# Expert gate rows from one-hot tables: float32 marks and one weighted product per token, against 16-bit marks and three products per token

## The reference, cut to what matters

```
q      = h @ wq                                  # 8 heads x 2 halves x 128
s1, s2 = q_half @ keys[head, half].T             # 128 key scores for each half
top 16 of s1, top 16 of s2; 256 sums; top 16 of the sums per head
w      = softmax(those 16 sums)                  # per head
expert = 128 * key1 + key2                       # 16384 experts, 128 picks per token
out    = sum over picks of  w * gelu(h . u[expert]) * v[expert]
```

## Time and profile before

| | before |
|---|---|
| median of 3 runs | 4277.51 us (4276.9 to 4279.27) |
| span of the profiled execution | 4272.1 us |
| TensorE matmul busy in it | 4130.4 us, 97% |
| VectorE busy in it | 3026.6 us, 71% |
| ScalarE busy in it | 1804.8 us, 42% |
| mean share of the DMA engines, query and selection tiles of the first call (1550 to 1720 us) | 0.67 |

### The profile page before, as it was taken

One profiled execution on the slowest core, in us unless ns is written; L12 is line 12 of the kernel. 1 busy time (PEld: TensorE's weight loads), 2 busy tenths in 40 slices (PEclk: granted clock), 3 DMA queues, 4 the chain that ended last, 5 costly groups with the idle time before them and its releaser, 6 DMA issues. The chain is left out here.

```text
span 4272.1 us, 80920 instructions
## 1 busy us (share of the span) xinstructions
PE 4130.4 (97%) x30455; PEld 3777.3 (88%) x30455; DVE 3026.6 (71%) x5239; ACT 1804.8 (42%) x2677; POOL 32.3 (1%) x54
## 2 busy tenths in 40 slices
PE   9999999999997899999999999999998899999999
PEld 9978999879895699999888899998886699999887
DVE  5566565565525479787888697878885579787888
ACT  4344343343324344444333444443333444444333
POOL 0000000000000000000000000000000000000000
PEclk9999999999999999999999999999999999999999
DMA  6534656436320157545776465457771156546776
GB/s 241 215 147 168 232 201 229 148 137 229 131 89 21 60 178 226 189 176 196 234 234 214 176 229 191 174 187 235 234 234 68 60 203 221 187 176 202 233 235 199
DMA packets 299140, 783.66 MB, mean 183 GB/s; under 512 B 33008, under 2 KB 132336, under 8 KB 298352
## 3 DMA queue, kind: packets, MB, share of 16 engines
q1 hardware_dynamic: 298864, 779.78, 53.4%
HBM read 728.27 MB, written 51.38 MB: 182 GB/s over the span
## 5 line engine op out<-in xcount | busy, mean ns | idle before, releaser
L262 ACT ACTIVATE ring_hi<-ring 128x1024 fp32r<-128x1024 f32 x1173 | 1244.7, 1061 | 2023.7 <-PE banks L283 1303.5
L268 DVE TENSOR_TENSOR ring_lo<-ring,ring_hi 128x1024 fp32r<-128x1024 f32 x1173 | 1436.9, 1226 | 624.3 <-ACT ring_hi L262 598.3
L279 PE MATMUL banks<-h_parts,ring_hi 128*128 128x256 f32 x4824 | 1208.0, 288 | 8.9 <-PEq L623 3.5
L280 PE MATMUL banks<-h_parts,ring_hi 128*128 128x256 f32 x4824 | 1182.3, 283 | 0.0
L279 PEld LDWEIGHTS banks<-h_parts,ring_hi 128*128 128x128 f32 x4824 | 923.0, 191 | 24.2 <-issue 22.1
L280 PEld LDWEIGHTS banks<-h_parts,ring_hi 128*128 128x128 f32 x4824 | 924.4, 192 | 0.8
L294 PE MATMUL banks<-h_parts,ring_hi 128*128 128x512 f32 x3048 | 764.6, 393 | 0.1
L283 PE MATMUL banks<-h_parts,ring_lo 128*128 128x256 f32 x4824 | 678.4, 283 | 3.9 <-DVE ring_lo L268 3.6
L294 PEld LDWEIGHTS banks<-h_parts,ring_hi 128*128 128x128 f32 x3048 | 548.7, 189 | 99.5 <-issue 1.3
L283 PEld LDWEIGHTS banks<-h_parts,ring_lo 128*128 128x128 f32 x4824 | 621.7, 192 | 8.6 <-DVE ring_lo L268 8.6
L297 PEld LDWEIGHTS banks<-h_parts,ring_lo 128*128 128x128 f32 x3048 | 416.5, 191 | 29.8
(11 more groups left out here) (234 smaller groups left out, 3781.6 us busy)
## 6 DMA issues: line engine op xcount, KB each, us to landing
ring<-peer_u_dram SPq DMA_DIRECT2D x384, 512.0 KB, 3.3
ring<-peer_v_dram SPq DMA_DIRECT2D x384, 512.0 KB, 3.7
big<-mod_w_dram SPq DMA_DIRECT2D x96, 512.0 KB, 4.3
act_store<-acts_out SPq DMA_DIRECT2D x384, 128.0 KB, 2.3
scratch<-act_store SPq DMA_DIRECT2D x384, 128.0 KB, 3.5
ring<-ffn_gate_dram SPq DMA_DIRECT2D x88, 512.0 KB, 3.7
ring<-ffn_up_dram SPq DMA_DIRECT2D x88, 512.0 KB, 3.2
ring<-ffn_down_dram SPq DMA_DIRECT2D x88, 512.0 KB, 3.2
```

Of the source, the lines that this page charges most:

```text
L262: self.nc.scalar.activation(self.hi[:, n % 2], self.ring[:, self.slot(j)], ACT.Copy).then_inc(self.count("tile_hi").sem, 1)
L268: self.nc.vector.tensor_tensor(self.lo[:, self.slot(j)], self.ring[:, self.slot(j)], self.hi[:, n % 2].bitcast(F32), ALU.subtract).then_in ...
L279: self.nc.tensor.matmul(out, w, b_hi, start=opens and m == 0, stop=False)
L280: self.nc.tensor.matmul(out, w, b_lo, start=False, stop=False)
```

## The change

The marks become bfloat16 and lie with the four tokens innermost: `marks[r, m, key, t]`, m = 0 to 3. `iota` shrinks to the 16 columns that `choose` needs, and a new constant `fours` (each key number four times, packed as bfloat16) takes its place. `picks` becomes bfloat16 with five rows: the two keys, and the softmax weight as a sum of three bfloat16 parts. The first part is ScalarE's copy, which rounds to 16 bits; `part_weights`, four instructions on VectorE once per call, makes the other two. `mark(n)` is three instructions: both one-hot tables (1024 elements), the second table times the first two parts (1024), and the second table times the third part (512). `gates(n)` makes three bfloat16 products for each token, added up in the bank, all with the table of the first key as the stationary operand.

```diff
-for _name, _n in (("ident", P), ("rot", P), ("iota", P), ("cos", T), ...
+for _name, _n in (("ident", P), ("rot", P), ("iota", TOPK), ("fours", 2 * P), ("cos", T), ...
...
-        self.picks = sb("picks", [P, 3, T])
+        self.picks = sb("picks", [P, 5, T], BF16)
...
-    marks = k.scratch[:].rearrange("p (r side t n) -> p r side t n", r=2, side=2, t=B)
-    iota = k.c("iota").unsqueeze(1).unsqueeze(1).to_broadcast([P, 2, B, NKEYS])
+    marks = k.scratch[:].bitcast(BF16).rearrange("p (r m n t) -> p r m n t", r=2, m=4, t=B)
+    keys_in_fours = k.c("fours").bitcast(BF16).rearrange("p (n t) -> p n t", t=B).unsqueeze(1).to_broadcast([P, 2, NKEYS, B])
+    rests = k.scratch[:, 0:2 * T].rearrange("p (r t) -> p r t", r=2)
...
                 for t in range(B):
-                    last = nc.tensor.matmul(k.ps[:, n % R, t * P:(t + 1) * P], marks[:, n % 2, 0, t], marks[:, n % 2, 1, t],
-                                            start=True, stop=True)
+                    for m in (0, 1, 3):
+                        last = nc.tensor.matmul(k.ps[:, n % R, t * P:(t + 1) * P], marks[:, n % 2, 2, :, t],
+                                                marks[:, n % 2, m, :, t], start=m == 0, stop=m == 3)
...
-                nc.vector.tensor_tensor(marks[:, n % 2], iota, k.picks[:, 0:2, at].unsqueeze(3).to_broadcast([P, 2, B, NKEYS]),
+                nc.vector.tensor_tensor(marks[:, n % 2, 2:4], keys_in_fours,
+                                        k.picks[:, 0:2, at].unsqueeze(2).to_broadcast([P, 2, NKEYS, B]),
                                         ALU.is_equal).then_inc(marked.sem, 1)
-                dve.wait_ge(marked.sem, marked.after(n + 1))
-                nc.vector.tensor_tensor(marks[:, n % 2, 1], marks[:, n % 2, 1],
-                                        k.picks[:, 2, at].unsqueeze(2).to_broadcast([P, B, NKEYS]),
+                dve.wait_ge(marked.sem, marked.after(2 * n + 1))
+                nc.vector.tensor_tensor(marks[:, n % 2, 0:2], marks[:, n % 2, 3:4].to_broadcast([P, 2, NKEYS, B]),
+                                        k.picks[:, 2:4, at].unsqueeze(2).to_broadcast([P, 2, NKEYS, B]),
+                                        ALU.mult).then_inc(marked.sem, 1)
+                dve.wait_ge(marked.sem, marked.after(2 * n + 2))
+                nc.vector.tensor_tensor(marks[:, n % 2, 3], marks[:, n % 2, 3],
+                                        k.picks[:, 4, at].unsqueeze(1).to_broadcast([P, NKEYS, B]),
                                         ALU.mult).then_inc(marks_weighted.sem, 1)
+
+            def part_weights():
+                turned = k.ps[:, 7, 0:T]
+                dve.wait_ge(picked.sem, picked.after(3))
+                nc.vector.tensor_tensor(rests[:, 0], turned, k.picks[:, 2], ALU.subtract).then_inc(parted.sem, 1)
+                ...
+                nc.vector.tensor_copy(k.picks[:, 3], rests[:, 0]).then_inc(parted.sem, 1)
+                ...
+                nc.vector.tensor_tensor(rests[:, 1], rests[:, 0], k.picks[:, 3], ALU.subtract).then_inc(parted.sem, 1)
+                ...
+                nc.vector.tensor_copy(k.picks[:, 4], rests[:, 1]).then_inc(parted.sem, 1)
...
-            dve.wait_ge(picked.sem, picked.after(3))
+            part_weights()
             for n in range(N - NS):
```

More of the change, by code:

```diff
@@ L59 @@
 CON = {}
-for _name, _n in (("ident", P), ("rot", P), ("iota", P), ("cos", T), ("sin", T), ("side", 10), ("row_pick", 30), ("rows_pick", 30)):
+for _name, _n in (("ident", P), ("rot", P), ("iota", TOPK), ("fours", 2 * P), ("cos", T), ("sin", T), ("side", 10), ("row_pick", 30), ("rows_pick", 30)):
     CON[_name] = (sum(n for _, n in CON.values()), _n)
@@ L80, in _constants @@
     put("rot", rot)
-    put("iota", np.broadcast_to(i, (P, P)))
+    put("iota", np.broadcast_to(i[:TOPK], (P, TOPK)))
+    in_fours = (np.repeat(i, 4).astype(np.float32).view(np.uint32) >> 16).astype(np.uint16)
+    put("fours", np.broadcast_to(in_fours.view(np.float32), (P, 2 * P)))
     put("side", i[:, None] % 32 == np.arange(10))
@@ L119 @@
     "window_sum", "window_mean", "pooled", "pool_product", "mods_biased", "key_scores", "key_scores_moved",
-    "top_step", "pair_scores", "first_keys_marked", "pick_step", "weight_exp", "picks_turned", "keys_marked", "marks_weighted", "gate_product", "gate_kept",
+    "top_step", "pair_scores", "first_keys_marked", "pick_step", "weight_exp", "picks_turned", "weight_parted", "keys_marked", "marks_weighted", "gate_product", "gate_kept",
     "gelu_done", "expert_weighted", "half_added", "picks_kept", "mod_product", "mod_product_kept", "mod_turned", "mod_kept", "lam_copied", "lam_products", "lam_exps", "lam_ready",
@@ L1700, in experts @@
         "picks_turned", "picks_kept"))
-    marked, marks_weighted, product, kept = map(k.count, ("keys_marked", "marks_weighted", "gate_product", "gate_kept"))
+    marked, marks_weighted, product, kept, parted = map(k.count, (
+        "keys_marked", "marks_weighted", "gate_product", "gate_kept", "weight_parted"))
     weighted, rounded, ready, summed, added = map(k.count, ("expert_weighted", "hidden_hi", "hidden_ready", "sums_complete",
@@ L1918, in mark @@
                 at = slice(n * B, (n + 1) * B)
-                nc.vector.tensor_tensor(marks[:, n % 2], iota, k.picks[:, 0:2, at].unsqueeze(3).to_broadcast([P, 2, B, NKEYS]),
+                nc.vector.tensor_tensor(marks[:, n % 2, 2:4], keys_in_fours,
+                                        k.picks[:, 0:2, at].unsqueeze(2).to_broadcast([P, 2, NKEYS, B]),
                                         ALU.is_equal).then_inc(marked.sem, 1)
-                dve.wait_ge(marked.sem, marked.after(n + 1))
-                nc.vector.tensor_tensor(marks[:, n % 2, 1], marks[:, n % 2, 1],
-                                        k.picks[:, 2, at].unsqueeze(2).to_broadcast([P, B, NKEYS]),
-                                        ALU.mult).then_inc(marks_weighted.sem, 1)
+                dve.wait_ge(marked.sem, marked.after(2 * n + 1))
[5 more added lines that the diff above has]
+                                        k.picks[:, 4, at].unsqueeze(1).to_broadcast([P, NKEYS, B]),
+                                        ALU.mult).then_inc(marks_weighted.sem, 1)
+            def part_weights():
+                turned = k.ps[:, 7, 0:T]
+                dve.wait_ge(picked.sem, picked.after(3))
+                nc.vector.tensor_tensor(rests[:, 0], turned, k.picks[:, 2], ALU.subtract).then_inc(parted.sem, 1)
+                dve.wait_ge(parted.sem, parted.after(1))
+                nc.vector.tensor_copy(k.picks[:, 3], rests[:, 0]).then_inc(parted.sem, 1)
+                dve.wait_ge(parted.sem, parted.after(2))
+                nc.vector.tensor_tensor(rests[:, 1], rests[:, 0], k.picks[:, 3], ALU.subtract).then_inc(parted.sem, 1)
+                dve.wait_ge(parted.sem, parted.after(3))
+                nc.vector.tensor_copy(k.picks[:, 4], rests[:, 1]).then_inc(parted.sem, 1)
+                dve.wait_ge(parted.sem, parted.after(4))
             def weigh(r, i, e, free):
@@ L2056, in experts @@
         c.ends(16 * (N // R))
-    for c in (marked, marks_weighted, product, kept):
+    marked.ends(2 * STEPS)
+    for c in (marks_weighted, product, kept):
         c.ends(STEPS)
+    parted.ends(4)
     scored.ends(HEADS)
```

## The result

| | before | after |
|---|---|---|
| median of the runs | 4277.20 us (4 runs, 4273.78 to 4279.27) | 4376.49 us (4 runs, 4371.8 to 4388.47) |
| profiled span | 4272.1 us | 4375.8 us |
| profiled execution's own time | not given | 4377.65 us |

The ratio is 1.0235, with a 95% interval of 1.0223 to 1.0247: the change makes the kernel 99 us slower, where I forecast 41 us faster. Shares by engine look the same on the page as before: TensorE is busy for 97% again, for 97 us more.

The account below looks back on a forecast made before the run. TensorE was taken to bound the stages with gates; 0.215 us saved per step over 3 calls x 64 steps is 41.3 us, so 4277.5 - 41.3 = 4236.2 us. Range 4230 to 4303 (0.83); the forecast's own, 4230 to 4246.

Parts of the forecast that it names:

- What bounds the kernel: Stages with gates: TensorE has no gap, so its time is the kernel's until VectorE's 0.68 us idle per step is used.
- What TensorE does instead: Gates: twelve bfloat16 matmuls at 0.056 us take 0.672 us instead of 0.887, gaining 0.215 us per step, 41.3 us in all.
- the unknown: Gates' new operands are not dense: a token's keys lie 8 bytes apart, for the load and the moving side.
- The bound from above: Gates' matmuls at the slowest pace seen, 0.111 us: twelve take 1.332 us, a step 0.445 us longer.
- Rival 2: Gates: TensorE turns load-bound or read-bound at 0.111 us per matmul, +85 us, 4363 us; chance 0.10.
- the 8-byte step being free: Gates' strided operands: accesses run at full rate as long as two fall in each line, as at 8 bytes.
- VectorE: Marks: three 16-bit instructions at two elements per cycle, 0.692, 0.692 and 0.419 us, leaving VectorE waiting half a microsecond each step.
- the prices at both paces: VectorE's marks: 1.225, 1.225 and 0.692 us at one element per cycle; 0.692, 0.692 and 0.419 at two.
- part_weights: Four VectorE instructions once per call, 1.5 us, covered before the first gates; uncovered, at most 4.5 us in all.
- The larger constants: Program start: 144 more columns, about 1.1 us more to load, covered by SyncE's 3.1 us wait for TensorE.

Follow-up runs that it names:

- the fix: The change with tokens in twos innermost (a token's keys 4 bytes apart) and picks laid out to match, against the kernel before: 4251.29 us, ratio 0.9938.

## Why the prediction was wrong, point by point

- **What bounds the kernel: right.** TensorE stays without a gap in these stages in the kernel before, in the changed one and in the fix, and 192 times the difference of the step is the difference of the time in each: 101 against 99 us, 27 against 27, (3.767 - 3.387) x 192 = 73 against 74.
- **What TensorE does instead: this step failed.** "I take 0.056, since it is the row with the same type, the same columns and the same loads." The row agreed in these, and differed in one that set the pace, the 8-byte step of the moving operand. I named that step as the unknown and then gave it no price. Measured: 0.118, and 0.058 once that read alone is dense. Twelve cost 1.414 us in the step (4.294 - 2.880), not 0.672.
- **The bound from above did not hold, and came close by luck.** I had 1.332 us from the pace of float32 weight loads, 0.111, and the real figure lies 6% above it. The load wasn't the cause: at 8-byte steps it stays hidden but for 0.002 us. The price belongs to the moving read, and has no ceiling at 0.111 (0.225 at 16 bytes). Rival 2, "load-bound or read-bound", at 4363 us with a chance of 0.10, is what happened in its read-bound form; the range left it out. 0.10 was too low for a property that no row of the trace showed.
- **The Trainium skill's rules.** The 81 ns per pair of load and matmul ("TensorE: Matmul & The Clock Gate", "Back-to-back issue gap") isn't seen here, neither dense (56 ns) nor strided (118). The rule of two accesses in each 16-byte line ("SBUF — State Buffer", "Specifications (TRN2)"), which I cited for the 8-byte step being free, is contradicted for TensorE's moving operand: at 8 bytes two elements fall in each line and the pace is half. The measurement decides.
- **VectorE: right**, in durations (692, 692, 425 ns) and in the prices at both paces. The rows of before had no 16-bit instruction with two inputs to rest this on. The Trainium skill's rule on two elements per cycle ("Vector Engine (DVE) Microarchitecture Reference", section 5.1) agrees with the trace in both directions: runs of four and of two adjacent elements run at 692 ns, an operand that stands still in the innermost dimension at 1225 ns.
- **`part_weights`: right to call it free.** From the last split under the selection to the first gates are 7.93 us before (1734.04 to 1741.97) and 7.94 after:

```profile
1736.23 1.23 DVE L271 TENSOR_TENSOR ring_lo<-ring,ring_hi 128x1024 fp32r<-128x1024 f32 x1 [1.65 <-ACT ring_hi L265]
1737.37 0.42 DVE L1942 TENSOR_TENSOR scratch<-banks,picks 128x256 f32<-128x256 f32 x1
...
1738.94 0.69 DVE L1925 TENSOR_TENSOR scratch<-con,picks 128x1024 bf16<-128x1024 bf16 x1
```

  The four instructions take 1.57 us (1.5 forecast) and TensorE shows no gap behind them; the first gates start at 1744.17.
- **The larger constants: right to call them free**, as far as the runs tell. After they land SyncE still waits 1.5 us for TensorE, where it waited 3.1. The kernel with 4-byte steps, which has the same constants, starts its first gates at 1742.20, against 1741.98 before.
- **A small term missed:** 0.055 us per step even with dense operands, 11 us in all. With it a dense version gains 31 us (3.767 - 3.607, times 192), not 41. It didn't show in the changed kernel, where twelve times 0.118 is the whole cost of gates.
- **A reading slightly off:** the rounded starts in the earlier trace rows are 3.76 us apart, not 3.765. The sum used 3.767, from the 63 intervals, so nothing follows from it.

## What to carry to other kernels

Price a matmul by the layout of its moving operand as well as by type and columns: for 16-bit data and 128 columns a step of 4 bytes was almost free, 8 bytes doubled the time and 16 bytes took four times as long, while the stationary operand could be strided by 8 bytes for about 0.002 us per matmul. A layout that interleaves rows to please VectorE should interleave no further than its pace needs (runs of two here). And where the best row differs from the new instruction in one property, that property, not the rest, deserves the chance; a stream that is "busy" at full clock hides such a read completely, so look at the distance between starts.

## What the runs showed of the hardware that I had not expected

- The moving read of a 16-bit matmul of 128 columns: 0.056 us dense, 0.058 at 4-byte steps, 0.088 at 6, 0.114 at 8, 0.225 at 16 (0.118 at 8 with the load strided too).
- The load of 128 x 128 16-bit weights at 8-byte steps stays almost hidden: the matmul's pace goes from 0.056 to 0.058 us.
- Behind a matmul of 0.111 us and behind one of 0.056, the second matmul of the next tile starts 0.23 us after the last one of gates.
- With reads at 16-byte steps the granted clock had a mean of 0.92 to 0.94 in the stages with gates, with short stretches at 0.50 and TensorE busy throughout.
- A float32 matmul of 128 columns reads its moving operand at 8-byte steps for 0.003 us more per record.
